# A two-block transformer kernel: its first weight tile loaded from ScalarE's queue, seven tables from GpSimd's, its last output block in halves

## The chip, the cores and the metric

The kernel runs on one core of one Trainium2 chip. The metric is the device time of one execution in microseconds (us). The kernel before takes 2472.11 us, the median of 3 runs (2471.87 to 2472.23).

## The reference, cut to what matters

One sequence of 256 rows and 2048 columns in float32 goes through three layers. The first has an attention over chunks with a relative bias and a differential attention, then a gated feed-forward part; the second has a latent attention over selected keys, then the same feed-forward; the third is a hybrid of a gated convolution and a windowed attention, and ends in a LayerNorm. Around the change two things matter:

```
h = rmsnorm(x, attn_norm[0])
p = h @ even_w_in[0]              # the first weight matrix, 2048 rows deep
...
y = einsum(y, w_out) + b_out
out = layer_norm(ALPHA * x + y, ln_g, ln_b)   # the end: 256 x 2048 float32
```

Small vectors enter as tables: attn_norm (2 x 2048), ffn_norm, final_norm, b_in, conv_b, conv_ln_g, conv_ln_b, b_subln, c_kv_norm, b_lambda, a_rel_bias, t5_table.

## The kernel before, in words

All instructions are written out by hand, engine by engine, with semaphores between them; no scheduler moves anything. Weights come from HBM in units of 512 KB (512 rows of 256 columns, or 256 rows of 512), into a ring of four buffers `raw`. ScalarE (ACT) copies each unit to the high half of a split (`hi`, L208), VectorE (DVE) subtracts to get the low half (`lo`, L214), and TensorE (PE) multiplies three products of halves (`mul_W`, L262). A buffer may be loaded again when `lo` of its unit is done; `load` waits for that on the semaphore `s_lo` (L219). For the first four units that semaphore is raised by DVE itself, by RING at the start of `setup_dve`, behind nine other increments.

The order of the start is this. SyncE (SP, `setup_sp`) issues the first half-slices of x (`xload0a`), the weight unit 0, the second half-slices, unit 1, and so on, each as two DMAs. ACT (`setup_act`) issues twelve DMAs of small tables into `rows`, 128 elements to a row: the first one, attn_norm[0], counts on the semaphore `rowsA`, the other eleven on `rowsB`. Then it splits unit 0 in halves (L557, L559), with `hs_hi` (L587), the high half of the normed x, between them. GpSimd (POOL, `setup_pool`) makes the identity matrix `ident` and issues four DMAs for the bias tables, on `rowsC`.

PE (`setup_pe`) runs 10 idle products of `ident` (L644), then waits for `rowsA` and turns that table (L652). DVE copies it to `gains` (L468), and both ACT's `hi` of x and DVE's `lo` of x (L594) need it. PE goes on with 7 idle products, the 4 transposes of x (`x_pe`, L639), 8 more idle products, and then the first real product (L262). After unit 1 it comes to `tables_pe` (L658 on), which waits for the other tables and turns them.

The end is a LayerNorm over two blocks of 128 rows. Its four functions are below. PE runs 24 idle products (L2109), turns one column (L2111), waits for ACT to copy the result (L2103), and multiplies a 2-row matrix into four banks of 512 columns (L2115). DVE finishes block 0 (L2154, four quarters), which takes nothing from these products, then block 1 (L2159, four quarters), whose quarter q needs bank q. SP sends each quarter, 256 KB, when DVE has written it (L2166).

Of the kernel before, what the change touches and what calls it, by code (L numbers as in the profile page):

```python
# [17 lines left out]
ACT, ALU = mybir.ActivationFunctionType, mybir.AluOpType  # L18
P = 128
D, S, FF = 2048, 256, 5632  # L20
# [48 lines left out]
def build(nc, a):  # L69
# [14 lines left out]
    xr = sb("x", [P, 2, D])  # L84
# [42 lines left out]
    rows = at("rows", [P, 3, P], F32, off[0])  # L127
# [10 lines left out]
    ident, ones = sb("ident", [P, P]), sb("ones", [P, P])  # L138
# [17 lines left out]
    PG = nc.alloc_psum_tensor("PG", [P, 4, 512], F32)  # L156
    PS = nc.alloc_psum_tensor("PS", [P, 2, 512], F32)
    PO = nc.alloc_psum_tensor("PO", [P, 2, 512], F32)
# [32 lines left out]
    def sem(name):  # L191
        name = shared(name)[0]
        if name not in sems:
            sems[name] = nc.alloc_semaphore(name)
        return sems[name]
# [20 lines left out]
    def load(e, seg, i, j, src, wide=0):  # L216
        e.wait_ge(s_lo, seg.unit(i, j) + 1)
        dst = raw[:, j % RING]
        if wide == 2:  # L219
            pair = dst.rearrange("p (k m) c -> p k m c", m=2)  # L220
            for m in (0, 1):
                e.dma_start(pair[:, :, m, :], src[m]).then_inc(s_raw[j % RING], 16)
            return
        if wide:
            dst = dst.rearrange("p (k m) c -> p k (m c)", m=2)
        e.dma_start(dst, src).then_inc(s_raw[j % RING], 16)
# [95 lines left out]
    gA = Seg(1, [8] * 6, [0, 2] * 3)  # L322
# [39 lines left out]
    def w(e, name, v):  # L362

        if not (isinstance(v, int) and v <= 0):
            e.wait_ge(sem(name), v + shared(name)[1])
# [9 lines left out]
    def pair_cols(W, j, c0):  # L375

        return [W.rearrange("(t p) n -> p t n", p=P)[:, 2 * j:2 * j + 2, c:c + UC] for c in (c0, c0 + 1024)]
# [34 lines left out]
    QT = D // 4  # L412
# [6 lines left out]
    def setup_sp(e):  # L419
        for c in range(4):  # L420
            if c == 0:
                x_load(e, 0, slice(0, QT // 2), "a")
            if c == 1:
                x_load(e, 0, slice(QT // 2, QT))
            if c == 2:
                x_load(e, 1)
            load(e, gA, 0, c, pair_cols(a["even_w_in"][0], c, 0), 2)
        x_load(e, 2)
        x_load(e, 3)
    tab = setm[0:20, 0, 0:32]  # L430
# [5 lines left out]
    def setup_pool(e):  # L436
        e.memset(ident[:], 0.0).then_inc(sem("id"), 1)
        e.memset(nat[:], 0.0).then_inc(sem("id"), 1)
        w(e, "id", 2)
        e.affine_select(out=ident[:], in_=ident[:], compare_op=ALU.not_equal, fill=1.0, base=0,  # L440
                        pattern=[[-1, P]], channel_multiplier=1).then_inc(sem("id"), 1)
        for t in (0, 1):
            e.dma_start(nat[:, t, 0:8], a["a_rel_bias"][0, t * P:(t + 1) * P, :]).then_inc(sem("rowsC"), 16)
        e.dma_start(nat[0:1, 2, 0:8], a["a_rel_bias"][0, 256:257, :]).then_inc(sem("rowsC"), 16)
        e.dma_start(nat[0:32, 3, 0:20], a["t5_table"]).then_inc(sem("rowsC"), 16)

    def bias_pool(e):
        w(e, "lines", 33)
# [83 lines left out]
    def back_to_front(t):  # L532
# [2 lines left out]
        v = t[:, :, n - 1:n]  # L535
        return bass.AP(tensor=v.tensor, offset=v.offset, ap=[list(v.ap[0]), list(v.ap[1]), [-1, n]])

    def setup_act(e):
        rise(e, "act")
        def table(part, n, at_row, src, name):  # L540
            e.dma_start(rows[at_row:at_row + n, part, :], src.rearrange("(t p) -> t p", p=P)).then_inc(sem(name), 16)
        table(0, KT, 0, a["attn_norm"][0], "rowsA")
        e.preload_act_table_set(LOG_EXP)
        table(1, KT, 0, a["attn_norm"][1], "rowsB")
        for l in range(2):
            table(1, KT, KT + KT * l, a["ffn_norm"][l], "rowsB")
        table(1, KT, 3 * KT, a["final_norm"], "rowsB")
        table(2, 42, 0, a["b_in_2"][0], "rowsB")
        table(2, 8, 42, a["conv_b_2"][0], "rowsB")
        table(2, 8, 50, a["conv_ln_g_2"][0], "rowsB")  # L550
        table(2, 8, 58, a["conv_ln_b_2"][0], "rowsB")
        table(2, 2, 66, a["b_subln"][0], "rowsB")
        table(2, 2, 68, a["c_kv_norm"][0], "rowsB")
        e.dma_start(rows[70:74, 2, :], a["b_lambda"][0]).then_inc(sem("rowsB"), 16)
        w(e, "tabD", 1)
        e.wait_ge(s_raw[0], 32)
        e.activation(ws[0][:, 0:2, 0, :], raw[:, 0, 0:2], ACT.Copy).then_inc(sem("half"), 1)  # L557
        slice_hi(e, 0, (0, 1))
        e.activation(ws[0][:, 2:4, 0, :], raw[:, 0, 2:4], ACT.Copy).then_inc(s_hi, 1)  # L559
        hi(e, 1, 1)  # L560
        slice_hi(e, 0, (2, 3))
        hi(e, 2, 2)
        squares(e, "n0", 0)
        slice_hi(e, 1)
        hi(e, 3, 3)
# [89 lines left out]
        keep_busy(e, 8)  # L655

    def tables_pe(e):
        w(e, "rowsB", 176)  # L658
        e.transpose(PO[:, 0, KT:5 * KT], rows[0:4 * KT, 1, :], ident[0:4 * KT, 0:4 * KT])
        e.transpose(PO[:, 0, 128:202], rows[0:74, 2, :], ident[0:74, 0:74]).then_inc(sem("tabT"), 1)  # L660
        w(e, "rowsC", 64)
        for t in range(4):
            ins = e.transpose(PO[:, 1, t * P:(t + 1) * P], nat[:, t, :], ident[:])
        ins.then_inc(sem("tabT"), 1)
# [1442 lines left out]
    def ln_pe(e):  # L2107
        for _ in range(24):
            e.matmul(PO[:, 1, 384:512], ident[:], ident[:], start=True, stop=True)  # L2109
        w(e, "rec", 13)  # L2110
        e.transpose(PO[0:1, 0, 0:P], moved, ident[:]).then_inc(sem("lnT"), 1)  # L2111
        w(e, "lnc", 1)
        w(e, "lnrow", 64)
        for q in range(4):
            e.matmul(PG[:, q, :], shift2[:], lnpair[:, q * QT:(q + 1) * QT], start=True, stop=True).then_inc(sem("lnu"), 1)  # L2115

    def ln_dve(e):
        w(e, "part", 8)
        w(e, "lnrow", 64)

        def centre(q):
            c = slice(q * D // 2, (q + 1) * D // 2)
            e.scalar_tensor_tensor(xr[:, 0, c], xr[:, 0, c], low[:, 0:1], lnrow[:, 0, c], ALU.add, ALU.mult).then_inc(sem("lf"), 1)
        e.reduce_sum(t, parts, axis=mybir.AxisListType.X).then_inc(sem("rec"), 1)
        w(e, "rec", 2)
        e.tensor_scalar(low, t, -1.0 / D, None, ALU.mult).then_inc(sem("rec"), 1)
        w(e, "rec", 3)
        w(e, "fs", 7)
        centre(0)
        w(e, "fs", 8)  # L2130
        e.tensor_tensor(gap, low, away, ALU.subtract).then_inc(sem("rec"), 1)
        e.reduce_sum(y, sqs, axis=mybir.AxisListType.X).then_inc(sem("rec"), 1)
        w(e, "rec", 4)
        e.tensor_tensor(gap, gap, gap, ALU.mult).then_inc(sem("rec"), 1)
        w(e, "rec", 6)
        e.scalar_tensor_tensor(v, y, 1.0 / D, gap, ALU.mult, ALU.subtract).then_inc(sem("rec"), 1)
        w(e, "rec", 7)
        e.tensor_scalar(v, v, LN_EPS, None, ALU.add).then_inc(sem("rec"), 1)
        row_gain(e, 3)
        steps = (lambda: e.tensor_tensor(t, v, y, ALU.mult),  # L2140
                 lambda: e.tensor_tensor(t, t, y, ALU.mult),
                 lambda: e.tensor_scalar(t, t, -0.5, 1.5, ALU.mult, ALU.add),
                 lambda: e.tensor_tensor(t, t, y, ALU.mult))
        w(e, "rsf", 1)
        for c, f in enumerate(steps):
            w(e, "rec", 8 + c)
            f().then_inc(sem("rec"), 1)
        w(e, "rec", 12)
        e.tensor_tensor(moved, t[:, 1:2], low[:, 1:2], ALU.mult).then_inc(sem("rec"), 1)
        centre(1)  # L2150
        for q in range(4):
            w(e, "lf", q // 2 + 1)
            c = slice(q * QT, (q + 1) * QT)
            e.scalar_tensor_tensor(xr[:, 0, c], xr[:, 0, c], t[:, 0:1], lnrow[:, 1, c], ALU.mult, ALU.add).then_inc(sem("fin"), 1)  # L2154
        w(e, "xg", 20)
        for q in range(4):
            c = slice(q * QT, (q + 1) * QT)
            w(e, "lnu", q + 1)
            e.scalar_tensor_tensor(xr[:, 1, c], xr[:, 1, c], t[:, 1:2], PG[:, q, :], ALU.mult, ALU.add).then_inc(sem("fin"), 1)  # L2159

    def ln_sp(e):
        for b in (0, 1):
            for q in range(4):
                c = slice(q * QT, (q + 1) * QT)
                w(e, "fin", 4 * b + q + 1)
                e.dma_start(a["out"][0, b * P:(b + 1) * P, c], xr[:, b, c]).then_inc(sem("out"), 16)  # L2166
        w(e, "out", 128)
    phase(sp=ln_sp, act=ln_act, dve=ln_dve, pe=ln_pe)

    with nc.Block() as block:  # L2170
# [40 lines left out]
```

## Time and profile before

| | us |
|---|---|
| median of 3 runs | 2472.11 |
| the profiled execution | 2472.14 |
| its span, first to last instruction | 2470.3 |
| what lies around the span | 1.84 |
| PE busy | 2461.3 |
| DVE busy | 1722.3 |
| ACT busy | 1204.5 |
| POOL busy | 59.6 |

The columns of a timeline are start, duration, engine, line, operation, output<-input, count, and in brackets the idle time before. "SPq", "ACTq" are issues of DMAs by the engine's sequencer; the duration is that of the issue, not of the transfer. "DMA to landing" runs from the start of the issue to the landing.

### The profile page before, as it was taken

What the parts mean: (1) busy time and instruction counts of PE and PEld (TensorE: products, weight loads), DVE (VectorE), ACT (ScalarE), POOL (GpSimd) and SP (SyncE); (2) the same over time, 40 slices, a digit from 0 to 9 for tenths busy, and PEclk for the clock granted to TensorE, in tenths of its full rate; (3) what the DMA queues carried; (4) which work ended last, traced back from release to release, by engine and by line L of the source; (5) the groups of instructions that cost most, each with busy time, mean ns of one, the idle gap of its engine ahead of it and who ended that gap; (6) DMA issues with size and microseconds to landing.
All of it is one profiled execution on the core that took longest, in us unless ns stands there. A gap on an engine that the chain in (4) does not pass through costs nothing.

```text
span 2470.3 us, 32210 instructions
## 1 busy us (share of the span) xinstructions
PE 2461.3 (100%) x11403; PEld 2043.8 (83%) x11403; DVE 1722.3 (70%) x2620; ACT 1204.5 (49%) x1588; POOL 59.6 (2%) x81
## 2 busy tenths in 40 slices
PE   9999999999999999999999999999999999999999
PEld 7888888888888888888888888888888888888777
DVE  7766786666666656667867666666666665889985
ACT  6454555444444444445555544444444444556773
POOL 1000000000000000000220000000000000100000
PEclk9999999999999999999999999999999999999999
DMA  7555556666666655557545666666665555765454
GB/s 245 183 175 182 172 176 197 192 193 194 188 196 194 194 192 194 196 167 216 164 144 173 195 195 191 192 195 194 193 191 194 196 192 193 224 181 169 145 192 141
DMA packets 284443, 463.16 MB, mean 187 GB/s; under 512 B 18221, under 2 KB 100863, under 8 KB 283832
## 3 DMA queue, kind: packets, MB, share of 16 engines
q1 hardware_dynamic: 282080, 453.64, 59.7%
q0 software_dynamic: 1984, 8.14, 1.0%
q8 instruction: 61, 1.00, 0.2%
q14 instruction: 38, 0.31, 0.0%
q10 hardware_dynamic: 280, 0.08, 0.0%
HBM read 459.65 MB, written 2.14 MB: 187 GB/s over the span
## 4 chain that ended last, share of the span: by engine, by line
PE 94%; DVE 3%; ACT 2%; issue 1%; POOL 0%; DVEq 0%; ACTq 0%; POOLq 0%
PE PG L262 85%; PE PG L238 3%; PE PG L237 1%; DVE ws L214 1%; DVE cacc L1560 1%; PE PO L905 1%; PE PS L848 1%; ACT ws L208 0%; PE PS L891 0%; PE PG L250 0%; PE PG L1337 0%; PE PS L849 0%; PE PO L906 0%; DVE pT L1230 0%; PE PO L1346 0%
## 5 line engine op out<-in xcount | busy, mean ns | idle before, releaser
L214 DVE TENSOR_TENSOR ws<-raw,ws 128x1024 fp32r<-128x1024 f32 x859 | 1053.1, 1227 | 670.7 <-ACT ws L208 664.0
L262 PE MATMUL PG<-ws,hs 128*128 128x512 f32 x6336 | 1455.3, 390 | 0.7 <-DVE hs L594 0.7
L208 ACT ACTIVATE ws<-raw 128x1024 fp32r<-128x1024 f32 x859 | 908.7, 1059 | 1065.2 <-PE PG L262 989.2
L262 PEld LDWEIGHTS PG<-ws,hs 128*128 128x128 f32 x6336 | 1185.0, 188 | 246.4 <-issue 1.1
L262 PE MATMUL PG<-ws,fs 128*128 128x512 f32 x2112 | 479.0, 389 | 0.0
L262 PEld LDWEIGHTS PG<-ws,fs 128*128 128x128 f32 x2112 | 396.5, 188 | 82.3
L262 PE MATMUL PG<-ws,os 128*128 128x512 f32 x1140 | 262.2, 390 | 1.0 <-DVE ws L214 1.0
L262 PEld LDWEIGHTS PG<-ws,os 128*128 128x128 f32 x1140 | 213.2, 188 | 45.8 <-DVE ws L214 1.8
L611 DVE STREAM_TRANSPOSE turnb<-qst 32x256 f32<-32x256 f32 x352 | 153.4, 436 | 7.2
L238 PE MATMUL PG<-hs,ws 128*128 128x512 f32 x368 | 128.7, 393 | 0.0
L1560 DVE SCALAR_TENSOR_TENSOR cacc<-hc,convw,cacc 128x256 f32<-128x256 f32 x232 | 100.1, 487 | 0.0
L237 PE MATMUL PG<-hs,ws 128*128 128x256 f32 x345 | 98.8, 286 | 0.1
L611 DVE STREAM_TRANSPOSE turnb<-x 32x256 f32<-32x256 f32 x192 | 83.7, 436 | 3.5
L238 PEld LDWEIGHTS PG<-hs,ws 128*128 128x128 f32 x368 | 68.3, 188 | 13.9 <-DVEq L1382 0.3
L237 PEld LDWEIGHTS PG<-hs,ws 128*128 128x128 f32 x345 | 65.1, 189 | 1.2 <-issue 0.4
L943 DVE STREAM_TRANSPOSE qk<-natqk 32x256 f32<-32x256 f32 x128 | 55.8, 436 | 9.6 <-ACT natqk L1129 7.5
L874 ACT ACTIVATE ts<-ts,small 128x256 f32<-128x256 f32 x96 | 42.4, 443 | 23.4 <-DVE small L866 23.4
L814 ACT ACTIVATE cross<-PG,small 128x512 f32<-128x512 f32 x44 | 27.8, 685 | 33.2 <-PE PG L262 33.2
L827 DVE SCALAR_TENSOR_TENSOR qst<-PG,small,cross 128x512 f32<-128x512 f32 x44 | 31.0, 747 | 9.6 <-PE PG L262 9.6
L580 ACT ACTIVATE cross<-x 128x512 f32<-128x512 f32 x40 | 25.3, 632 | 11.3 <-DVE x L762 9.3
L791 ACT ACTIVATE fs<-turnb 128x1024 f32 (+1 forms) x22 | 23.3, 1061 | 15.2 <-DVE turnb L611 15.2
L795 DVE TENSOR_TENSOR fs<-turnb,fs 128x1024 f32 (+1 forms) x22 | 26.8, 1218 | 0.0
(311 smaller groups left out, 909.2 us busy)
## 6 DMA issues: line engine op xcount, KB each, us to landing
raw<-in_w_gate SPq DMA_DIRECT2D x176, 512.0 KB, 4.0
raw<-in_w_up SPq DMA_DIRECT2D x176, 512.0 KB, 4.3
raw<-in_w_down SPq DMA_DIRECT2D x176, 512.0 KB, 3.6
raw<-in_even_w_in SPq DMA_DIRECT2D x128, 256.0 KB, 3.0
raw<-in_w_in SPq DMA_DIRECT2D x52, 512.0 KB, 3.6
raw<-in_odd_w_in SPq DMA_DIRECT2D x44, 512.0 KB, 3.7
raw<-in_even_w_in SPq DMA_DIRECT2D x32, 512.0 KB, 3.7
raw<-in_even_w_out SPq DMA_DIRECT2D x32, 512.0 KB, 4.5
```

Source lines behind the costliest of these rows:

```text
L208: e.activation(ws[j % RING][:, :, 0, :], raw[:, j % RING], ACT.Copy).then_inc(s_hi, 1)
L214: e.tensor_tensor(w[:, :, 1, :], raw[:, j % RING], w[:, :, 0, :].bitcast(F32), ALU.subtract).then_inc(s_lo, 1)
L237: e.matmul(PG[:, bank + c, 0:S], wl, rhs[:, k0 + kk, 0, :], start=False, stop=False)
L238: ins = e.matmul(PG[:, bank + c, :], wh, both, start=st, stop=end)
L262: ins = e.matmul(out[:, b, :], x_, w[:, kk, :, h, :], start=first and kk == 0 and n == 0, stop=last and kk == 1 and n == 2)
L611: return e.transpose(blocks_out, blocks_in)
L795: e.tensor_tensor(fs[:, bass.ds(4 * i, 4), 1, :], turnb[:], fs[:, bass.ds(4 * i, 4), 0, :].bitcast(F32), ALU.subtract).then_inc(sem(p + "f ...
L814: ins = e.activation(sil[:, b], gates[:, b, :], ACT.Silu, scale=rnT[:, b:b + 1])
L827: ins = e.scalar_tensor_tensor(nat_f[:, b], ups[:, b, :], rnT[:, b:b + 1], sil[:, b], ALU.mult, ALU.mult)
L874: e.activation(ts[:, h, src], ts[:, h, src], ACT.Exp, bias=nmx[:, n:n + 1], accum_out=sm[:, n:n + 1]).then_inc(sem(p + "e"), 1)
L943: ins = e.transpose(blocks_out, blocks_in)
L1560: e.scalar_tensor_tensor(dst, hc[:, n, c:c + S], convw[:, n, c:c + 1], dst, ALU.mult, ALU.add).then_inc(sem("cv"), 1)
```

## The change

ACT issues the two DMAs of weight unit 0, ahead of its tables; SP leaves them out, so that everything behind them in SP's order moves up by two. Seven of ACT's twelve tables are issued by POOL behind its own four, and count on `rowsC`, not on `rowsB`. `tables_pe` waits for all of both ahead of its first transpose. At the end PE runs two more idle products, between the turn of the column and the wait for ACT's copy; and the last quarter of block 1 is finished by DVE and sent by SP as two pieces of 256 columns.

```diff
@@ setup_sp
-            load(e, gA, 0, c, pair_cols(a["even_w_in"][0], c, 0), 2)
+            if c:
+                load(e, gA, 0, c, pair_cols(a["even_w_in"][0], c, 0), 2)
@@ setup_pool
+        table_row(e, 2, 42, 0, a["b_in_2"][0], "rowsC")
+        table_row(e, 2, 8, 42, a["conv_b_2"][0], "rowsC")
+        table_row(e, 2, 8, 50, a["conv_ln_g_2"][0], "rowsC")
+        table_row(e, 2, 8, 58, a["conv_ln_b_2"][0], "rowsC")
+        table_row(e, 2, 2, 66, a["b_subln"][0], "rowsC")
+        table_row(e, 2, 2, 68, a["c_kv_norm"][0], "rowsC")
+        e.dma_start(rows[70:74, 2, :], a["b_lambda"][0]).then_inc(sem("rowsC"), 16)
@@ before setup_act
+    def table_row(e, part, n, at_row, src, name):
+        e.dma_start(rows[at_row:at_row + n, part, :], src.rearrange("(t p) -> t p", p=P)).then_inc(sem(name), 16)
@@ setup_act
+        load(e, gA, 0, 0, pair_cols(a["even_w_in"][0], 0, 0), 2)
         table(0, KT, 0, a["attn_norm"][0], "rowsA")
...
-        table(2, 42, 0, a["b_in_2"][0], "rowsB")
...
-        e.dma_start(rows[70:74, 2, :], a["b_lambda"][0]).then_inc(sem("rowsB"), 16)
@@ tables_pe
-        w(e, "rowsB", 176)
+        w(e, "rowsB", 64)
+        w(e, "rowsC", 176)
...
-        w(e, "rowsC", 64)
@@ ln_pe
         e.transpose(PO[0:1, 0, 0:P], moved, ident[:]).then_inc(sem("lnT"), 1)
+        for _ in range(2):
+            e.matmul(PO[:, 1, 384:512], ident[:], ident[:], start=True, stop=True)
         w(e, "lnc", 1)
@@ ln_dve
-        for q in range(4):
-            c = slice(q * QT, (q + 1) * QT)
+        for q, c in ((0, slice(0, QT)), (1, slice(QT, 2 * QT)), (2, slice(2 * QT, 3 * QT)), (3, slice(3 * QT, 3 * QT + 256)), (3, slice(3 * QT + 256, D))):
             w(e, "lnu", q + 1)
-            e.scalar_tensor_tensor(xr[:, 1, c], xr[:, 1, c], t[:, 1:2], PG[:, q, :], ALU.mult, ALU.add).then_inc(sem("fin"), 1)
+            u = PG[:, q, c.start - q * QT:c.stop - q * QT]
+            e.scalar_tensor_tensor(xr[:, 1, c], xr[:, 1, c], t[:, 1:2], u, ALU.mult, ALU.add).then_inc(sem("fin"), 1)
```

`ln_sp` sends nine pieces instead of eight, each when `fin` has counted it.

ACT's program from its first instruction stands so before (`rows` are the tables, `ws` the split weights):

```order
L541 DMA rows<-in_attn_norm 16x128
L543 ACT_TABLE_LOAD
L541 DMA rows<-in_attn_norm 16x128
L541 DMA rows<-in_ffn_norm 16x128 x2
L541 DMA rows<-in_final_norm 16x128
L541 DMA rows<-in_b_in 42x128
L541 DMA rows<-in_conv_b 8x128
L541 DMA rows<-in_conv_ln_g 8x128
L541 DMA rows<-in_conv_ln_b 8x128
L541 DMA rows<-in_b_subln 2x128
L541 DMA rows<-in_c_kv_norm 2x128
L554 DMA rows<-in_b_lambda 4x128
```

ACT's program from its first instruction stands so in the changed kernel, with the wait of its first DMA for `s_lo`:

```order
L222 DMA raw<-in_even_w_in 128x2x256 [waits lo]
L222 DMA raw<-in_even_w_in 128x2x256
L547 DMA rows<-in_attn_norm 16x128
L555 ACT_TABLE_LOAD
L547 DMA rows<-in_attn_norm 16x128
L547 DMA rows<-in_ffn_norm 16x128 x2
L547 DMA rows<-in_final_norm 16x128
```

The table that PE waits for, the first of attn_norm, moves from the first place of ACT's order to the third, behind two DMAs of 256 KB.

POOL's program behind the making of the identity stands so in the changed kernel (before, `lines` follows `in_t_table` at once):

```order
L444 DMA nat<-in_a_rel_bias 128x8 x2
L445 DMA nat<-in_a_rel_bias 1x8x1
L446 DMA nat<-in_t_table 32x20
L547 DMA rows<-in_b_in 42x128
L547 DMA rows<-in_conv_b 8x128
L547 DMA rows<-in_conv_ln_g 8x128
L547 DMA rows<-in_conv_ln_b 8x128
L547 DMA rows<-in_b_subln 2x128
L547 DMA rows<-in_c_kv_norm 2x128
L453 DMA rows<-in_b_lambda 4x128
L457 DMA lines<-setm 8x384
```

Seven DMAs join POOL's order between its own four and the first that needs a result of DVE.

PE's program at its end stands so before, from the last product of a full unit on:

```order
L262 MATMUL PG<-ws_85,os 128x512 x12
L272 MATMUL PG<-ws_86,os 128x512 x12
L2109 MATMUL PO<-ident 128x128 x24
L2111 MATMUL PO<-ident,small 1x128
L2115 MATMUL PG<-lnpair,shift_81 128x512 x4
```

PE's program at its end stands so in the changed kernel:

```order
L262 MATMUL PG<-ws_85,os 128x512 x12
L272 MATMUL PG<-ws_86,os 128x512 x12
L2114 MATMUL PO<-ident 128x128 x24
L2116 MATMUL PO<-ident,small 1x128
L2118 MATMUL PO<-ident 128x128 x2
L2122 MATMUL PG<-lnpair,shift_81 128x512 x4
```

The two products of L2118 stand where PE waited for ACT's copy.

## Rows read from the trace of the kernel before

**Rows 1.** The waits of PE over the whole run: total us, times, longest.

```profile
PE PO L1791 <- ACT pT L898: 1.1, 1, 1.1
...
PE PG L262 <- DVE hs L594: 0.7, 1, 0.7
```

**Rows 2.** The chain of waits of the start: start us, us, what.

```profile
2.00 2.39 PE PO L644 x10
4.40 0.21 PE PO L652
4.61 1.69 PE PO L644 x7
6.30 0.46 PE PS L639 x4
...
8.28 1.63 PE PG L262 x6
...
15.37 0.20 PE PO L659
```

**Rows 3.** The timeline of the start, every engine.

```profile
0.75 0.87 SPq L417 DMA_DIRECT2D x<-in_x  x2
0.88 0.40 ACTq L541 DMA_DIRECT2D rows<-in_attn_norm  x1
...
1.67 0.94 SPq L222 DMA_DIRECT2D raw<-in_even_w_in  x2
...
3.91 0.53 POOL L445 DMA_DIRECT2D nat<-in_t_table  x1
...
5.89 0.63 ACT L557 ACTIVATE ws<-raw 128x512 fp32r<-128x512 f32 x1 [3.29 <-DMA raw<-in_even_w_in]
...
7.65 0.88 DVE L594 SCALAR_TENSOR_TENSOR hs<-PS,gains,hs 128x256 fp32r<-128x256 f32 x2 [0.32 <-ACT hs L587]
```

**Rows 4.** DMAs by issuing line: durations of issue in ns, then us to landing.

```profile
L541 ACTq DMA_DIRECT2D rows<-in_attn_norm x1: 401/401/401, 0.9 to 0.9; - x1
...
DMA to landing us min/median/max: 2.4/2.4/2.4
...
L222 SPq DMA_DIRECT2D raw<-in_even_w_in x1: 470/470/470, 2.1 to 2.1; - x1
...
DMA to landing us min/median/max: 3.4/3.4/3.4
...
L445 POOL DMA_DIRECT2D nat<-in_t_table x1: 533/533/533, 3.9 to 3.9; - x1
...
DMA to landing us min/median/max: 3.9/3.9/3.9
```

**Rows 5.** A stretch of the start: busy by engine, granted clock, DMA share, GB/s.

```profile
0.00:2.00 2.00, 0.00 (x0) 0.00 (x0) 0.17 (x1) 0.68 (x1) 1.16 (x7) 1.00 0.07 16
```

**Rows 6.** The chain of waits of the end.

```profile
2461.50 0.28 ACT shift L2103
...
2461.82 5.30 PE PG L2115 x8
```

**Rows 7.** The timeline of the end, DVE and SP.

```profile
2464.52 2.06 DVE L2159 SCALAR_TENSOR_TENSOR x<-x,small,PG 128x512 f32<-128x512 f32 x3
...
2467.15 0.75 DVE L2159 SCALAR_TENSOR_TENSOR x<-x,small,PG 128x512 f32<-128x512 f32 x1 [0.57 <-PE PG L2115]
...
2467.92 0.33 SPq L2166 DMA_DIRECT2D out_y<-x  x1
```

**Rows 8.** Stretches of the end: PE, PEld, DVE, ACT, POOL busy, clock, DMA.

```profile
2461.82:2463.75 1.93, 1.93 (x5) 0.95 (x6) 1.93 (x4) 0.00 (x0) 0.00 (x0) 1.00 0.12 47
...
2464.00:2467.15 3.15, 3.11 (x4) 0.67 (x2) 2.58 (x4) 0.00 (x0) 0.00 (x0) 0.50 1.02 381
...
2468.25:2468.50 0.25, 0.00 (x0) 0.00 (x0) 0.00 (x0) 0.00 (x0) 0.00 (x0) 0.50 0.31 107
...
2468.75:2469.50 0.75, 0.00 (x0) 0.00 (x0) 0.00 (x0) 0.00 (x0) 0.00 (x0) 0.50 0.92 350
```

More of the change, by code:

```diff
@@ L540, in table @@
         def table(part, n, at_row, src, name):
-            e.dma_start(rows[at_row:at_row + n, part, :], src.rearrange("(t p) -> t p", p=P)).then_inc(sem(name), 16)
+            table_row(e, part, n, at_row, src, name)
+        load(e, gA, 0, 0, pair_cols(a["even_w_in"][0], 0, 0), 2)
         table(0, KT, 0, a["attn_norm"][0], "rowsA")
@@ L547, in setup_act @@
         table(1, KT, 3 * KT, a["final_norm"], "rowsB")
-        table(2, 42, 0, a["b_in_2"][0], "rowsB")
[L549 to L553, printed above, removed]
-        e.dma_start(rows[70:74, 2, :], a["b_lambda"][0]).then_inc(sem("rowsB"), 16)
         w(e, "tabD", 1)
@@ L2155, in ln_dve @@
         w(e, "xg", 20)
-        for q in range(4):
-            c = slice(q * QT, (q + 1) * QT)
+        for q, c in ((0, slice(0, QT)), (1, slice(QT, 2 * QT)), (2, slice(2 * QT, 3 * QT)), (3, slice(3 * QT, 3 * QT + 256)), (3, slice(3 * QT + 256, D))):
             w(e, "lnu", q + 1)
-            e.scalar_tensor_tensor(xr[:, 1, c], xr[:, 1, c], t[:, 1:2], PG[:, q, :], ALU.mult, ALU.add).then_inc(sem("fin"), 1)
+            u = PG[:, q, c.start - q * QT:c.stop - q * QT]
+            e.scalar_tensor_tensor(xr[:, 1, c], xr[:, 1, c], t[:, 1:2], u, ALU.mult, ALU.add).then_inc(sem("fin"), 1)
     def ln_sp(e):
+        done = 0
         for b in (0, 1):
[L2163 to L2167, printed above, removed]
+            for c0, c1 in ((0, QT), (QT, 2 * QT), (2 * QT, 3 * QT), (3 * QT, D)) if b == 0 else ((0, QT), (QT, 2 * QT), (2 * QT, 3 * QT), (3 * QT, 3 * QT + 256), (3 * QT + 256, D)):
+                done += 1
+                w(e, "fin", done)
+                e.dma_start(a["out"][0, b * P:(b + 1) * P, c0:c1], xr[:, b, c0:c1]).then_inc(sem("out"), 16)
+        w(e, "out", 16 * done)
     phase(sp=ln_sp, act=ln_act, dve=ln_dve, pe=ln_pe)
```

## The prediction, made before the changed kernel ran

> **What bounds the kernel now.** I read the list of PE's waits over the whole run first, then the chain of waits, then the timelines of the first 16 and the last 15 us, then the landings of single DMAs, and last the granted clock in short stretches. The reader is to see in the waits that PE never waits for a transfer, and that its longest wait between start and end is 1.1 us [rows 1]. So the time is PE's work, plus what lies ahead of its first real product and behind its last. A shift of the first product moves the end by as much, since nothing in the middle has slack to take it up; and the middle is unchanged. The whole question is two short stretches.
>
> At the start, the chain is PE's own pace: 10 idle products from 2.00 us, the turn of attn_norm at 4.40, 7 idle products, 4 transposes of x from 6.30 to 6.76, then one `hi` on ACT and one `lo` on DVE, and the first real product at 8.28 [rows 2]. No DMA ends a wait on it. The weight unit 0 releases ACT at 5.89, and ACT's half copy of 0.63 us is over at 6.52, 0.24 us before the transposes are [rows 2, 3]. The table attn_norm is issued by ACT at 0.88 and lands 2.4 us later, at 3.28 [rows 3, 4]; PE comes to it at 4.40, so it has 1.1 us of slack.
>
> At the end, the last link is: PE's eight half-products from 2461.82 to 2467.12 [rows 6], DVE's last quarter from 2467.15 to 2467.90, its DMA issued at 2467.92 [rows 7], its bytes moved from 2468.75 for 0.92 x 0.75 = 0.7 us, until 2469.45 [rows 8], and 0.85 us to the span's end at 2470.3. The half-products begin at full clock and end at half: 1.93 us at a granted clock of 1.00 (2.4 GHz), then 3.15 us at 0.50 (1.2 GHz), in which DVE waits 0.57 us for the last one [rows 7, 8].
>
> **The start: unit 0 issued by ACT.** What it can give: unit 0 earlier. That is worth nothing, as ACT's copy of it already ends before the transposes, and PE's pace sets these. SP's later DMAs are issued 0.94 us sooner [rows 3], but none of them is on the chain.
>
> What it costs: the table attn_norm goes behind two DMAs. First its issue. ACT's first load waits for `s_lo`, which DVE raises at the end of its ten increments. SP passed the same wait at 1.67 without a visible stop, so it is raised by then; ACT itself is ready at 0.88 [rows 3]. The load starts between 0.88 and 1.67; I take 1.5, near the upper end, since ACT's two increments cost it 0.13 us against SP's 0.75 start and DVE has five times as many, and more for slower ones. Two issues of 0.47 us [rows 3] put the table's issue at 2.45 (bounds 1.83 and 2.62).
>
> Then its landing. In an empty queue it took 2.4 us [rows 4]. Now 512 KB stand ahead of it in the same queue. The nearest row is SP's second DMA of unit 0, behind 512 KB in its own queue: 3.4 us [rows 4]. Bounds: 2.4 us if the small DMA is not held by the large ones, and 4.4 us, one more us, if SP's x and unit 1, which now run beside unit 0, halve its pace. I take 3.4: 2.45 + 3.4 = 5.85. PE comes to it at 4.40 and the turn then starts 1.45 us late; from there to the first real product every link is in series (7 products, transposes, ACT, DVE). The cost is +1.5 us; bounds 1.83 + 2.4 = 4.23, which is 0, and 2.62 + 4.4 = 7.0, which is +2.6. Unit 0 itself lands at the same time or sooner than the table, and the copy has 2.15 us to spare then (7 products and 4 transposes), so it costs nothing beside it.
>
> The Trainium skill bears on this in "DMA: Bandwidth & Descriptors", section "Issuing engines are not separate DMA queues": DMAs from different engines interleave on the same 16 DMA engines, and issuing from several only saves the sequencer's time. By that rule the 0.94 us of SP's time is all that is saved, and no byte comes sooner; the trace before shows the engines at a share of 0.07 in the first 2 us [rows 5], so it neither shows nor denies it for these two queues together.
>
> **The seven tables on POOL.** ACT's issues shrink, off the chain. On POOL the last issue of before ends at 4.44 [rows 3]; seven more of 0.53 us are 3.7 us, to 8.15, and with 3.9 us to landing [rows 4] the tables are there at 12.1. PE asks for them at 15.37 [rows 2], or 1.5 us later with the shift. Cost 0 with 3 us of cover or more; if an issue or a landing takes 3 to 5 us longer, what is over comes on the path one for one. POOL's next step waits for DVE far later. 0 us.
>
> **Two idle products in the end.** A product of this kind takes 2.39 / 10 = 0.24 us [rows 2]; PE is done with the column 0.02 us before ACT's copy begins at 2461.50 and ACT is done at 2461.78 [rows 6]. Two take 0.48, so the half-products start at 2461.96 and not at 2461.82: +0.14 us on PE. What they may give is the clock. If it falls at the same moment as before, the delay doubles (+0.14 at full clock is +0.28 at half), and the last quarter starts at 2467.4. If it falls 0.48 us later, the sum is 0.28 - 0.48 = -0.2. If it doesn't fall, the 5.30 us of the half-products [rows 6] lose half of the 3.2 at half clock, PE ends at 2461.96 + 3.7 = 2465.7 and DVE sets the pace: its last quarter starts at 2466.58, when the three before are done [rows 7], 0.57 earlier.
>
> The Trainium skill, "TensorE: Matmul & The Clock Gate", section "What's actually happening", has a monitor set the clock by how busy PE has been, so a busy PE keeps it. By that rule alone filling the gap of 0.3 us would hold the clock and give the 0.57 us. The trace disagrees: the clock fell after 1.93 us without a pause in the two-row products [rows 8], so being busy with these is not enough, and I give the rule half.
>
> **The last quarter in halves.** Two operations of 256 columns take 0.88 us by the nearest row (L594 on DVE, two in 0.88) [rows 3] against 0.75 [rows 7]: +0.13. The transfer of the last piece is 128 KB and not 256: the stretch in which only the last piece moves is 0.7 us [rows 8], half is -0.35. Issue of the first half hides in DVE's second. With the clock as before: +0.25 +0.13 -0.35, about 0. With the clock held, DVE ends at 2466.58 + 0.88 = 2467.46, but the DMA engines are full (share 1.02) with the earlier blocks until 2468.33 (0.31 of the quarter us from 2468.25) [rows 8], and the last 256 KB need 0.7 behind them, so the bytes end at 2469.03 instead of 2469.45: -0.4. The end gives between 0.0 and -0.45; I take -0.2.
>
> **Sum** on the profiled execution: 2472.14 + 1.5 + 0 - 0.2 = 2473.4 us. Its time stands 0.03 above the median of the runs, so the median goes to 2473.4 too. The bound for telling a difference, 0.2%, is 4.9 us here: this is "the same".
>
> **The rivals.**
> 1. The table is not held. If the load's wait is over near 0.9 and the small DMA slips past the large ones, it lands at 4.2 to 4.9 us, and the start costs 0 to 0.5. For it: ACT is free at 0.88, and the landing of 2.4 us is mostly latency. Against: the landing grew by one us where 512 KB stood ahead [rows 4]. With the end: -0.45 to +0.5, say 2472.0. Chance 0.22.
> 2. Both large DMAs share their pace with SP's and the table lands at 6.5 or later: +2.1 to +3.3 at the start. For it: both queues run on the same DMA engines, and SP's next 768 KB then stand beside unit 0, not behind it. Time 2474.6. Chance 0.13.
> 3. The change does not do what it says in the end: two idle products do not hold the clock. That alone is +0.2 on the sum, inside each case above.
> 4. The other side: PE, waiting for the table behind its first 10 products, loses its clock, and the first real products run at 1.2 GHz. Place: from the turn of attn_norm on. Price: one us for each us of full-clock work run at half; with 1.3 us from the shift it needs 3.6 us of such work, that is more than the first unit (2 x 1.63 us [rows 2]), to pass 4.9. For it: the clock fell in the end behind a gap of 0.3 us and thin work. Against: PE stood idle for the first 2.0 us at a granted 1.00 [rows 5]. Time 2477.5. Chance 0.04.
>
> **How the numbers follow.** The main case has 0.58, with its own range of 2472.6 to 2474.2; rival 1 has 0.22, rival 2 0.13, rival 4 0.04, and 0.03 are for what I don't see, in the tables on POOL among it. All but rival 4 and some of the rest are within 4.9 us. A gain of over 4.9 us has no place to come from: the time without a full PE is some 9 us in all. So slower 0.05, faster 0.01, same 0.94. The range of 8 in 10 runs from rival 1's middle to rival 2's: 2471.8 to 2475.0.
>
> **What would show it.** Right: PE waits for attn_norm's turn between 4.4 and 5.9 us, released by a DMA of ACT's queue; the first L262 starts near 9.8; PE runs on without a wait behind it, L659 at about 16.9; the last bytes move before 2471. Wrong: a turn at 4.4 and a first product at 8.3 (rival 1), a granted clock of 0.5 before 15 us (rival 4), PE idle ahead of L659 (the tables on POOL), or a first product earlier than 8.28, which by my reading nothing can bring.

## The result, and the profile after

The changed kernel takes 2475.97 us, the median of 20 runs (2475.16 to 2476.94), against 2472.30 us of before in 20 runs (2471.87 to 2473.76): a ratio of 1.0014, interval 1.0008 to 1.0021. It is 3.7 us slower. I forecast 2473.4 and a range from 2471.8 to 2475.0; it lies 1 us beyond the upper end.

The profiled execution has a span of 2474.5 us, 4.2 us longer than before's 2470.3, and took 2476.33 us. The waits of PE over the whole run name the place at once (total us, times, longest). The first row has no counterpart in [rows 1], the second has:

```profile
PE PO L657 <- DMA rows<-in_attn_norm: 4.1, 1, 4.1
...
PE PO L1796 <- ACT pT L903: 1.1, 1, 1.1
```

The chain of waits of the start, which answers to [rows 2]:

```profile
1.60 0.03 DVEq L473
1.63 0.02 issue
1.66 0.46 ACTq L222
2.11 0.03 issue
2.14 0.49 ACTq L222
2.63 0.03 issue
2.66 5.82 DMA rows<-in_attn_norm
8.47 0.04 issue
8.52 0.28 PE PO L657
8.80 1.69 PE PO L649 x7
10.49 0.87 PE PS L644 x4
...
12.88 1.62 PE PG L262 x6
```

Read backwards: the first real product starts at 12.88 us, 4.60 later than before. The turn of attn_norm starts at 8.52 and not at 4.33 (where before's timeline has it), 4.19 later, because the table's DMA took 5.82 us to land. That DMA was issued at 2.66, behind two DMAs of unit 0, which themselves waited until 1.66 for DVE's increment of `s_lo` (L473). The other 0.41 us is in the transposes of x: 0.87 us for four here, 0.46 before [rows 2].

The rest of the shift is small. By 28 us 0.25 us has come back: the group of twelve products that stood at 20.12 before stands at 24.47 here, 4.35 later, and the group ahead of it took 3.00 us before and takes 2.78 here. The end gives 0.33 (experiment 9). No other long wait of PE is new. POOL's tables cost nothing: the last of them was issued at 7.4 and landed 5.3 us later, at 12.7, and their turn (L665) follows the products before it without a gap at 19.96.

The single DMAs of the start, by their issuing line, as in [rows 4]: first the second DMA of unit 0, then attn_norm.

```profile
L222 ACTq DMA_DIRECT2D raw<-in_even_w_in x1: 488/488/488, 2.1 to 2.1; - x1
...
DMA to landing us min/median/max: 6.2/6.2/6.2
...
L547 ACTq DMA_DIRECT2D rows<-in_attn_norm x1: 487/487/487, 2.7 to 2.7; - x1
...
DMA to landing us min/median/max: 5.8/5.8/5.8
```

The second half of unit 0 lands 6.2 us after its issue where it took 3.4 on SP's queue [rows 4]. Both times differ from one execution to the next: over all profiles of this document the same DMA took 3.4 to 4.4 us on SP's queue, and 4.3 to 6.2 on ACT's with SP busy beside it. The view of the DMA queues from 2.5 to 5.5 us (packets, MB, share of the time of the 16 DMA engines; q1 is SP's, q10 ACT's, q0 POOL's) shows what happened:

```profile
DMA packets 808, 0.76 MB, mean 252 GB/s; under 512 B 70, under 2 KB 808, under 8 KB 808
...
q1 hardware_dynamic: 428, 0.39, 49.3%
q10 hardware_dynamic: 378, 0.37, 38.6%
q0 software_dynamic: 2, 0.00, 0.3%
```

The bytes are dealt out almost evenly between the two queues. In the kernel before, SP's queue had nearly all of the same 3 us:

```profile
q1 hardware_dynamic: 859, 0.81, 89.4%
```

There unit 0 had only the first half-slices of x ahead of it; now nearly every KB of it is matched by a KB of the second half-slices or of unit 1, which PE needs later. Both queues together also moved less, 0.76 MB against 0.86; why is not shown. And attn_norm, 8 KB that everything waits for, stands last.

### The profile page after: what moved, and what is told of

It is laid out like the page before. It is cut to its first block, busy times and chain, and to the rows that moved or that the text cites. A ratio compares the mean times of both kernels' runs of the same rounds, so it can differ in the third digit from the quotient of the medians.

```text
span 2474.5 us, 32221 instructions
## 1 busy us (share of the span) xinstructions
PE 2461.2 (99%) x11407; PEld 2044.7 (83%) x11407; DVE 1722.8 (70%) x2621; ACT 1204.3 (49%) x1588; POOL 63.0 (3%) x88
## 3 DMA queue, kind: packets, MB, share of 16 engines
HBM read 459.65 MB, written 2.14 MB: 187 GB/s over the span
## 4 chain that ended last, share of the span: by engine, by line
PE 93%; DVE 4%; ACT 2%; issue 1%; DMA 0%; DVEq 0%; ACTq 0%
PE PG L262 85%; PE PG L238 3%; PE PG L237 1%; DVE ws L214 1%; DVE cacc L1565 1%; PE PO L910 1%; PE PS L853 1%; ACT ws L208 0%; PE PS L896 0%; PE PG L250 0%; PE PG L1342 0%; PE PO L911 0%; PE PS L854 0%; DVE pT L1235 0%; PE PO L1351 0%
```

## The experiments

Theory S: the two hardware queues share the DMA engines by halves, so unit 0 on ACT's queue lands late, and the table behind it. Its rivals are named in the expectations. Each edit is against the kernel named ahead of it, and each ratio is against the kernel before, run beside it: 2472.34 us for experiments 1 to 4, 2472.52 for 5 to 8, 2472.44 for 9 to 11.

**1. Changed kernel, unit 0 back on SP.**

```diff
-            if c:
-                load(e, gA, 0, c, ...)
+            load(e, gA, 0, c, ...)
@@ setup_act
-        load(e, gA, 0, 0, ...)
```

> The changed kernel with unit 0 back in SP's order and the table attn_norm first on ACT; the seven tables on POOL, the two products and the halves stay. Theory S (two queues share the DMA engines by halves, so unit 0 on ACT's queue lands as late as one MB, and the table behind it): the table lands near 3.3 us again, the first real product starts at 8.3 and not at 12.9, and the time is 2472.3 less the 0.3 of the end, 2472.0. Rival P (POOL's seven DMAs slow every landing): first product still 1 us or more late, 2473.3 or more. It also shows whether the clock of the end holds again: if the two products did it, the half-products take 3.8 us and not 5.3.

Measured: 2472.85 us (10 runs), ratio 1.0002, 0.9993 to 1.0012. The loss is gone, and rival P, which wanted 2473.3 or more, is out: the seven tables on POOL are not the cause. But the first product starts at 8.72, not at the 8.3 of theory S. The chain of the start says what this is:

```profile
6.30 0.85 PE PS L642 x4
7.16 1.56 PE PO L647 x8
8.72 1.60 PE PG L262 x6
```

PE comes to x at 6.30 as before, but the four transposes take 0.85 us, not 0.46, and the idle products behind them are slow too. That is the pace of PE, not a landing (experiment 7 comes back to it). This run alone does not say why unit 0 on ACT's queue costs so much; experiment 4 does.

**2. Kernel before, unit 0 alone moved to ACT.**

```diff
+            if c:
+                load(e, gA, 0, c, ...)
@@ setup_act
+        load(e, gA, 0, 0, ...)
         table(0, KT, 0, a["attn_norm"][0], "rowsA")
```

> The kernel before with only unit 0 moved to ACT's queue ahead of the twelve tables. Theory S: table lands near 8.5 us, PE waits 4 us for it, first product near 12.9, time 2472.3 + 4.5 = 2476.8 (nothing given back in the end). Rival P: without POOL's tables the landing is near my forecast of 5.9, first product at 9.8, 2473.8. The end runs without the two products: half-products 5.3 us if these are what holds the clock.

Measured: 2475.62 us (10 runs), ratio 1.0014, 1.0004 to 1.0024. The one moved load makes nearly the whole loss, 3.3 us of 3.7. The chain in this kernel:

```profile
2.66 4.75 DMA rows<-in_attn_norm
7.41 0.05 issue
7.46 0.28 PE PO L654
```

The table lands after 4.75 us here and after 5.82 in the changed kernel. POOL's tables need not be the reason for the difference: the changed kernel, run once more (experiment 11), had 5.05.

**3. Changed kernel, attn_norm ahead of unit 0 on ACT.**

```diff
-        load(e, gA, 0, 0, ...)
         table(0, KT, 0, a["attn_norm"][0], "rowsA")
+        load(e, gA, 0, 0, ...)
```

> The changed kernel with attn_norm issued ahead of unit 0 on ACT's queue. Theory S: the table lands near 3.3 and PE is ready with x at 6.8, but unit 0 lands near 8.8, so ACT's half copy starts near 9 and the first product 2.1 us later near 11; time about 2472.0 + 2.7 = 2474.7. Rival R (only the table's place behind unit 0 costs, unit 0 itself is on time at 5.5 to 6): first product at 8.3 to 8.6, time 2472.0 to 2472.3.

Measured: 2472.66 us (10 runs), ratio 1.0001, 0.9991 to 1.0010. It lies between theory S (2474.7) and rival R (2472.0 to 2472.3), much nearer to R. The chain:

```profile
2.13 5.00 DMA raw<-in_even_w_in
7.14 0.02 issue
7.16 0.02 ACTq L561
7.18 0.05 issue
7.22 0.64 ACT ws L562
...
9.25 1.61 PE PG L262 x6
```

Unit 0 lands at 7.14. On SP's queue it landed at 5.5 in before's profile and at 6.5 in that of experiment 7, whose start is the same. In this profile the first product starts 0.5 to 1 us later than in those with unit 0 on SP's queue (8.28 to 8.72). So sharing delays unit 0, but S overstated it for this order (8.8), since I took it from a single execution; the larger part of the loss, 3.3 us of the medians, is the table's place behind unit 0.

**4. Changed kernel, SP waits for unit 0.**

```diff
             if c == 1:
+                e.wait_ge(s_raw[0], 32)
                 x_load(e, 0, slice(QT // 2, QT))
```

> The changed kernel with SP waiting for unit 0 to land before it issues the second half-slices of x and all behind it. Theory S: with nothing beside it in SP's queue unit 0 lands near 5.5, the table by 5.9, first product near 9.9, time about 2473.6, up to 1 us more if the later x and units now come late. Rival Q (a large load on ACT's queue is slow by itself, whoever else runs): the table still lands near 8.5, first product near 12.9, time 2476 or more.

Measured: 2475.31 us (10 runs), ratio 1.0011, 1.0001 to 1.0020. This run separates theory S (the neighbour slows unit 0) from rival Q (ACT's queue is slow by itself). The landings of unit 0's second DMA and of attn_norm:

```profile
L222 ACTq DMA_DIRECT2D raw<-in_even_w_in x1: 483/483/483, 2.1 to 2.1; - x1
...
DMA to landing us min/median/max: 3.5/3.5/3.5
...
L548 ACTq DMA_DIRECT2D rows<-in_attn_norm x1: 486/486/486, 2.6 to 2.6; - x1
...
DMA to landing us min/median/max: 3.3/3.3/3.3
```

The queues of this kernel from 2.5 to 5.5 us:

```profile
q10 hardware_dynamic: 669, 0.56, 58.8%
q1 hardware_dynamic: 153, 0.13, 15.6%
```

With SP held back, unit 0 on ACT's queue lands in 3.5 us, as it did on SP's, and the table behind it in 3.3, which is what I had forecast (3.4). PE turns the table at 6.03 and starts its first product at 10.39. So ACT's queue is not slow; its neighbour makes it so, by 1.7 to 2.5 us for the table (its turn is at 7.75 and 8.52 in the two profiles of the changed kernel). The time is not won, 2475.31 against an expected 2473.6 to 2474.6. At 19.65 PE is 3.4 us behind before's place for the same product (16.24): 2.1 us of this stand at the first product, 0.3 are slow first products (1.97 us for six, 1.63 before), and 0.85 are a wait, since SP's own stream is now late. The chain of this kernel holds that piece: unit 2, which ACT must copy before it turns to what PE waits for.

```profile
8.98 6.83 DMA raw<-in_even_w_in
15.81 0.02 issue
15.84 1.06 ACT ws L208
```

**5. Changed kernel, ACT's load without its wait for DVE.** The two `dma_start` of `load` stand in `setup_act` without the `wait_ge` on `s_lo`; the buffer has no earlier reader, so the wait protects nothing here.

> The changed kernel, with ACT's load of unit 0 not waiting for the semaphore that DVE raises (the buffers are unused then). The load starts at 0.9 and not at 1.66, the table is issued near 1.85 and not at 2.66. Theory S (landing is set by shared bytes, of which fewer are ahead): table lands 0.8 to 2 us earlier than 8.5, first product 11 to 12, time 2474 to 2475.2. Rival: the landing is set by SP's stream alone and does not move, 2476.

Measured: 2474.28 us (10 runs), ratio 1.0008, 0.9998 to 1.0017; by the medians 1.7 us less than the changed kernel, and its slowest run (2474.72) lies below that kernel's fastest (2475.16). The chain:

```profile
1.87 4.27 DMA rows<-in_attn_norm
...
10.71 1.73 PE PG L262 x6
```

The table is issued 0.79 us earlier and lands at 6.14, 4.27 us after its issue and not 5.05 or 5.82. So the wait for a semaphore that DVE raises last of ten was part of the cost, and it works twice: the issue is later, and the landing takes longer. That the latter comes from SP's bytes being ahead by then is my reading; no run shows it alone.

**6. Kernel before, the seven tables on POOL.** The edit is the change's own in `setup_pool`, `setup_act` and `tables_pe`.

> The kernel before with only the seven tables on POOL. Theory: they land by 13 us, ahead of 15.4, ACT and PE don't see them: 2472.3. Rival W (they slow the landing of x and unit 0, or shift when TensorE comes to its full pace, as the unit-0-on-SP kernel's 8.72 us for the first product and 2472.85 hint): first product 8.7 or later and 2472.7 or more.

Measured: 2472.71 us (11 runs), ratio 1.0001, 0.9992 to 1.0010: no difference that can be told. By the letter both signs of rival W came true, a first product at 8.70 and a time of 2472.7. But before itself stood at 2472.52 beside it, and the profile of experiment 9, whose start is that of before with no table on POOL, has the four transposes at the same slow pace and its first product at 8.69. So neither sign speaks against POOL.

**7. Kernel before, the two products of the end.**

```diff
         e.transpose(PO[0:1, 0, 0:P], moved, ident[:]).then_inc(sem("lnT"), 1)
+        for _ in range(2):
+            e.matmul(PO[:, 1, 384:512], ident[:], ident[:], start=True, stop=True)
```

> The kernel before with only the two idle products of the end. Theory C (the clock of the end falls at a moment that differs from run to run, products or not): 2472.3 to 2472.5, at most 0.1 above before from the 0.12 us by which the half-products start later. Rival H (the products hold the clock): 2471.9, and the half-products take 3.8 us in this profile.

Measured: 2472.52 us (11 runs) against 2472.52, ratio 1.0000, 0.9991 to 1.0009. In its profile the half-products took 3.70 us, all at full clock, as rival H has it, but the time is that of theory C: no gain. The timeline of the start of this kernel, whose start is before's, shows the pace of PE:

```profile
2.00 2.39 PE L644 MATMUL PO<-ident 128*128 128x128 f32 x10 [2.00 <-POOL ident L440]
...
4.54 1.59 PE L644 MATMUL PO<-ident 128*128 128x128 f32 x7
5.97 0.60 PE L639 MATMUL PS<-ident,x 128*128 128x128 f32 x4
```

Ten idle transposes of `ident` take 2.39 us, 0.24 each; four transposes of x take 0.60 from the first start to the last end, and 0.46 in before's chain, 0.11 each [rows 2]. It is the same operation at half and at full pace, 1.2 and 2.4 GHz, though the granted clock of the profile reads 1.00 from the first microsecond on. Where full pace comes differs from one execution to the next: here at about 5.7 us, in the profiled run of before at about 6.3, in that of experiment 1 after 8.

In this profile it is not PE's pace that sets the first product, at 8.65, but the landing of unit 0 on SP's queue, at 6.54:

```profile
2.14 4.40 DMA raw<-in_even_w_in
```

So the start of before, read from several profiles, has its first product between 8.28 and 8.69, and the 8.28 of the profile that I predicted from is the earliest of them. The 4.60 us at the first product, read against it, are thus the upper end; against 8.69 they are 4.2.

**8. Kernel before, the last quarter in halves.** The edit is the change's own in `ln_dve` and `ln_sp`.

> The kernel before with only the last quarter in two pieces. If the clock holds to the end, the bytes of the output are one unbroken stream of 5.45 us behind the first issue and the halves give nothing; if it falls early, the last piece is 0.35 us shorter to move and 0.12 later to be ready. So 2472.1 to 2472.3. Rival D (nine issues and pieces of 1 KB cost more than they save): 2472.4 or more.

Measured: 2472.61 us (11 runs) against 2472.52, ratio 1.0001, 0.9992 to 1.0010. I had expected 2472.1 to 2472.3, and by the letter it is rival D's number (2472.4 or more); against before in the same round it is 0.1 us, nothing that can be told.

**9. Kernel before, both edits of the end.**

> The kernel before with both edits of the end and the old start. Theory O (the end is the output's stream: 2 MB at 385 GB/s behind the first issue, so that neither edit moves it unless the clock falls early): from the first issue to the last byte 6.3 to 6.5 us, and 2472.3 to 2472.5. Rival: the two together give the 0.3 to 0.5 us that I forecast, 2472.0 with a time below before's in most runs.

Measured: 2472.44 us (11 runs) against 2472.44, ratio 1.0000, 0.9991 to 1.0009. As theory O has it, 6.48 us pass from the first issue of the output to the last byte. This number can be read in every profile, from the start of SP's row of the end to the last quarter of a microsecond in which the DMA engines still have a share:

| kernel | half-products us | halves | first issue to last byte us |
|---|---|---|---|
| before | 5.29 | no | 6.81 |
| 2 | 3.74 | no | 6.38 |
| 6 | 4.86 | no | 6.40 |
| 7 | 3.70 | no | 6.38 |
| changed | 3.77 | yes | 6.48 |
| 1, 3, 4, 5, 8, 9, 10, 11 | 3.69 to 4.48 | yes | 6.47 to 6.50 |

Where the clock falls late in the half-products, or behind them, the eight quarters leave in one unbroken stream, and the end is that stream: 2 MB at 385 GB/s are 5.4 us, and about 1 us to start. Only before's profiled run, with the clock falling early, had a hole in it (share 0.31, [rows 8], then 0 for a quarter of a microsecond). Where the stream has no hole, the halves add 0.1 us (6.38 to 6.40 without them, 6.47 to 6.50 with).

**10. Changed kernel, attn_norm first and unit 0 behind it without the wait.** The edits of 3 and 5 together: the best start with unit 0 on ACT that the runs point to.

> The changed kernel with attn_norm issued first on ACT and unit 0 behind it without the wait for DVE's semaphore: the best start with unit 0 on ACT that the runs point to. By the shared bytes unit 0 (issued at 1.3 and 1.8) lands near 6.1, ahead of 7.1 with the wait: first product near 8.5, time 2472.2 to 2472.6, no better than before. Rival (two queues at once bring the first bytes sooner, and the wait was what spoiled it): unit 0 lands by 5.2, and PE's pace alone sets 8.3 with 2471.9 or less.

Measured: 2472.27 us (11 runs) against 2472.44, ratio 1.0000, 0.9991 to 1.0010. ACT has unit 0 at 6.27; the first product starts at 8.70, set by PE's own pace:

```profile
4.40 0.21 PE PO L659
4.62 1.69 PE PO L651 x7
6.30 0.87 PE PS L646 x4
...
8.70 1.63 PE PG L262 x6
```

The whole loss is undone with unit 0 still on ACT's queue, and nothing is won over before.

**11. The changed kernel once more.**

> The changed kernel once more, for the spread of the landing from one execution to the next: the table again lands 4 to 6 us after its issue at 2.66, first product 11.8 to 13, time 2475.2 to 2476.9.

Measured: 2476.19 us, one run. The landing took 5.05 us, the first product started at 12.28 in the chain, and its six ran slowly: full pace came even later.

```profile
2.66 5.05 DMA rows<-in_attn_norm
...
9.72 0.85 PE PS L644 x4
10.57 1.71 PE PO L649 x8
12.28 2.04 PE PG L262 x6
```

So the table came 0.8 us sooner than in the first profile of this kernel, and the time is the same within 0.15 us: the sum of landing and pace is what counts.

## Why the prediction was wrong

**What bounds the kernel:** right in the main. The middle took up 0.25 of the 4.60 us by 28 us, and nothing behind it: the shift was 4.35 us there and 4.39 at the last unit.

**The table goes behind unit 0, and PE waits for it:** the mechanism was right, with its place and its releaser. **The size was not, and this is the step that failed: "I take 3.4: 2.45 + 3.4 = 5.85."** The issue was at 2.66 (bound 2.62, since ACT's load started at 1.66 and not at 1.5), and the landing took 5.8 us, against an upper bound of 4.4. That bound priced the sharing at "one more us". Of the 2.7 us by which the turn came later than forecast (4.19 and not 1.45), 2.4 are the landing and 0.2 the issue. The row of 3.4 us came from a queue that had the engines nearly for itself, and experiment 4 gives back 3.3 under that condition. With two queues at even shares 512 KB need the time of 1 MB. By my estimate another 512 KB at the 252 GB/s of those microseconds are 2.1 us on top of 3.4, 5.5 in all; the three profiles with the table issued at 2.66 behind unit 0 and SP running beside it measured 5.82, 5.05 and 4.75. Rival 2 named the sharing and gave it 0.13, with 2474.6, which is 1.4 us too low for the same reason. Which part of the delay comes from SP's later loads being issued two places sooner, and which from their standing beside unit 0 at all, no run separates.

In the Trainium skill, "DMA: Bandwidth & Descriptors", section "Issuing engines are not separate DMA queues", DMAs of different engines interleave on the same 16 DMA engines, and a second issuer saves only issue time. The traces agree, with 0.39 and 0.37 MB in the same 3 us, and they show the other side of it: here the interleaving took the share from what was needed first.

**Unit 0 earlier is worth nothing:** it wasn't earlier at all, but later: its second DMA took 6.2 us. Behind the table this did not show (ACT's half copy waited for the table too); in experiment 3 it did. I also misread where unit 0 stood before. It landed at 5.5 (2.14 + 3.4), and ACT began its copy at 5.89 because it issued its tables until 5.79; in experiment 1, with seven tables less, ACT began at 5.61. This changes nothing in the sum, since PE's pace came last, but the cover of unit 0 was smaller than I thought in executions such as that of experiment 7.

**The clock at the start:** missed. I read a granted 1.00 over PE's idle first 2 us [rows 5] as full clock and priced only a loss of it. The ten idle products at 0.24 us each [rows 2] say half pace, against 0.11 for the same operation later. In the profiles in which PE did not wait for the table full pace came between about 5.7 and 8.6 us, in the changed kernel's two, with a pause of 4.1 and 3.4 us, at about 12.4 and 13, by the time that the idle and the first real products took. In experiment 11 even the first real products still ran slowly (2.04 us for six, 1.63 before). That the pause is what puts it off fits these rows, but no run shows it alone. The 0.41 us on the transposes of x is no sign of it: five of the eight profiles without the pause have it too. In the Trainium skill, "TensorE: Matmul & The Clock Gate", section "What's actually happening", the throttled state is the default and activity releases it; the pace of the products agrees, the granted clock in the rows of the start doesn't show it. The pace is at most a part of the 3.7 us, not the cause: experiments 1, 6 and 9 have slow transposes too and lose nothing that can be measured.

**POOL's tables at 0:** right, with the last landing at 12.7 where I forecast 12.1.

**The end at -0.2:** the profiled runs give -0.33 from first issue to last byte (6.81 to 6.48), but I had the reason half wrong, and against the medians the term is 0. The clock did hold almost to the end of the half-products, 3.77 us. It also held without the two products in experiments 2 and 8 (3.74, 3.69). With them the half-products took 3.69 to 4.48 us in nine profiles, without them 3.69 to 5.29 in four; whether they help is left open, too few profiles. The prices of both edits were too high: the half-products start 0.34 us behind the start of ACT's copy and not 0.32, so the two products cost 0.02 us and not 0.14, and DVE's two halves take 0.78 us against 0.75 for one quarter, 0.03 more and not 0.13. In the medians neither edit nor both gave anything (experiments 7 to 9). The table shows why: in twelve of thirteen profiles the output's stream runs to its end without a hole. The profile of before that I worked from had an early fall of the clock, and a gain against it is no gain against the median.

**The sum** of the profiled runs: +4.19 for the turn, +0.41 for the pace, -0.25 given back by 28 us, +0.04 to the last unit, -0.33 in the end, +0.13 from last byte to span's end: 4.2 us, as measured.

## What to carry to other kernels

Moving a load to a second hardware queue did not bring it sooner here; it got half of the bytes moved while the first queue had bytes waiting, and what stood behind it on the second queue inherited the delay. A few KB that a whole chain waits for belong first on their queue, ahead of any bulk load (experiment 3 wins 3.3 us by this alone), and an issue that waits for another engine's semaphore is itself a late issue. Take a landing time from a row only together with what else was in flight in that row, and look at more than one execution: the same DMA took 3.4 to 4.4 us in kernels with the same order of loads on SP's queue.

## What the runs showed of the hardware

- Two hardware queues with waiting transfers of 1 KB rows moved 0.39 and 0.37 MB in the same 3 us. An 8 KB table took 2.4 us to land in an empty queue, 3.3 behind 512 KB with the other queue nearly still, and 4.3 to 5.8 behind 512 KB with the other queue busy (4.27 in experiment 5, 4.75 in 2, 5.05 in 11, 5.82 in the first profile of the changed kernel).
- At the start of the program PE ran at half pace (0.24 us a transpose of 128 x 128, later 0.11) while the granted clock read 1.00; full pace came at about 5.7 us in one profile (experiment 7) and at about 13 in another (experiment 11).
- In the end the clock fell while PE was busy without a pause, with products of a two-row operand: 2.0 us into them in the profile of before, 3.5 us in the changed kernel, and only behind their end in five others (experiments 1, 5, 7, 8, 11).
